# A decoder trunk on one Trainium2 core: three page buffers in the compression, and the attention projection with its narrow block first and its sample rows in halves

## The chip, the cores and the metric

The kernel runs on one core of one Trainium2 chip. The metric is the device time of one execution in microseconds. The core's engines work side by side and meet in semaphores: PE (TensorE, matrix products and transposes), ACT (ScalarE), DVE (VectorE), POOL (GpSimd) and SP (SyncE, which here only issues DMAs). ACT issues some DMAs as well, in the order of its own program.

## The reference

One layer of a decoder for 1024 prompt rows and 64 sample rows (8 sequences of 8 new tokens). What the change touches is the first projection and the compression of keys and values:

```python
z = rms_norm(x, norm1_g) @ w_in          # 1024 -> 1304 attention columns + 1664 RWKV columns
# attention columns: q (512) | 3 branches x (k, v) (768) | gates (24)

def compress_blocks(kv, cmp_pe, cmp_w):  # blocks of 32 tokens, stride 16
    chunks = kv[:, :n_chunks * 16].reshape(B, n_chunks, 16, 2, 2, 64)
    for i in range(2):
        part = chunks[:, i:i + n_cmp] + pe[:, i]
        comp = comp + einsum('bnscgd,csde->bncge', part, w[:, i])
```

`compress_blocks` is computed for the prompt (63 blocks) and for each of the 8 sample sequences over its 2048 cached tokens (127 blocks), whose 16 pages of 128 tokens lie scattered in a pool and are found through `page_table`. After that come the attention of the prompt and of the samples, the output projection and an MLP; the RWKV part (time mixing in chunks) lies between the projection and the compression.

## The kernel before

**Projection.** The 1088 rows of x are 9 tiles (`TILES`): 8 of 128 rows and one, number `PT` = 8, of 64 sample rows. For each tile SP loads x (`load_x`), ACT normalises it (`norm_rows`, two buffers `xn`), PE turns it in 8 transposes into PSUM banks 0 and 1 (`turn_x`), and DVE copies it out into `nt` (semaphore `nt_out`, L2023). The attention columns of `w_in` are three blocks (`BLOCKS`, L506): two of 512 columns and one of 280. `ATT` lists 27 groups, block by block and in a block tile by tile; `att_group` (L1320) computes one as 8 products over the contraction, `nt` stationary and the weights moving, into one of three PSUM banks, and ACT copies it to `za` (`att_out`, L917 to L926). SP loads blocks 0 and 1 at the start (`load_w`), block 2 into the buffer of block 0 once its 9 groups are done. PE's program runs the turns of tiles 0 and 1, then the groups of block 0 with one turn ahead of each, and then the rest. The head norms of DVE and ACT (`head_sums`, `head_scale`, `head_norm`) need all three blocks of a tile and run beside the third block and the first groups of the RWKV columns (`rw_group`), which follow.

**Compression.** It runs over `CSEQ`: step k = 0 is sample sequence 1, step 1 the prompt, steps 2 to 8 the other samples, each in two halves a (keys, values), so 18 halves (`CHALF`). The pages of a step are loaded into one of two page buffers, `page_rows[k % 2]`: even pages by SP (`load_pages`, L652), odd ones by ACT (`odd_pages`, L1125 to L1135, four pages at a time). DVE splits them into heads (`split_heads`, L2260 to L2266, two halves ahead), PE transposes (`cm_turn`, L1622), DVE and ACT copy the result to `xt` (`x_copy`, L2273 and L1112), PE multiplies with the weights (`cm_product`) and adds neighbours (`cm_select`), ACT stores keys and values (`kv_copy`). A page buffer is free once the heads of the step that used it before are split (`cm_heads`). ACT issues the odd pages of step k + 2 at the end of its work for the halves of step k. The second buffer is the place of sample states that SP has to store first (`stored`). `mixed` holds the attention output in its first four rows of tiles, empty at this point, and the RWKV output in the other four.

Each engine works through its program in order, and all waits are on counts of progress.

## Time and profile before

| | us |
|---|---|
| median of 3 timed runs | 2261.91 (2259.36 to 2263.99) |
| the profiled execution | 2249.74 |
| its span, first to last instruction | 2248.0 |
| PE busy | 2115.9 (94%) |
| DVE busy | 1128.7 (50%) |
| ACT busy | 628.5 (28%) |
| POOL busy | 150.7 (7%) |

PE's mean granted clock over the span was 0.979 of full speed. In the names of operations, `arena` is the large SBUF buffer in which nearly all tiles lie; a line number leads to the code. L1299 is the helper of all matmuls, so these are told apart by shape: 128*64 is the stationary operand (rows * columns), 128x512 the moving one. A float32 product appears as two instructions, so a group of 8 products is x16. In a timeline, rows of the same kind are merged (x4), the second number is their length together, and the bracket is the idle time of the engine before them. In a chain of waits, the second number is the share of time that the piece holds up the chain.

### The profile page before, as it was taken

The numbers are of one execution on the slowest core, as the hardware profiler recorded it, in microseconds if no ns is written. First come the engines' busy times: TensorE is split into PE (matmuls) and PEld (weight loads), VectorE is DVE, ScalarE is ACT, GpSimd is POOL, SyncE is SP. The second block draws the span as 40 slices with busy tenths as digits, with TensorE's granted clock in tenths as the row PEclk, the third lists the DMA queues.
The fourth block names the chain that finished last, engine by engine and source line by source line (L and its number), as shares of the span: only waits on it lengthen the run. The fifth ranks groups of instructions, "written<-read, shape, count | busy, mean of one in ns | idle before, by whom it ended". The sixth has DMA issues, their size and how long they took to land.

```text
span 2248.0 us, 36929 instructions
## 1 busy us (share of the span) xinstructions
PE 2115.9 (94%) x15228; PEld 1199.6 (53%) x15228; DVE 1128.7 (50%) x2278; ACT 628.5 (28%) x1408; POOL 150.7 (7%) x248
## 2 busy tenths in 40 slices
PE   7999999899998887888887899999999999999999
PEld 4456566799996774444344444444444444444443
DVE  2026664367665446766545313463636354554635
ACT  4113553222322115666543311202020111111110
POOL 3000000122222001211110000000000000000000
PEclk9999999999998997999998999999999999999999
DMA  6000112100012531000035421011111111111101
GB/s 189 21 1 19 29 29 88 68 4 22 4 23 77 170 96 54 10 5 5 5 113 154 129 75 61 11 60 42 38 38 38 38 38 38 38 38 38 38 38 80
DMA packets 99957, 115.72 MB, mean 51 GB/s; under 512 B 32243, under 2 KB 72116, under 8 KB 99726
## 3 DMA queue, kind: packets, MB, share of 16 engines
q1 hardware_dynamic: 95310, 106.01, 15.0%
q10 hardware_dynamic: 4480, 7.34, 1.1%
q8 instruction: 121, 1.98, 0.4%
q14 instruction: 46, 0.38, 0.1%
HBM read 104.75 MB, written 12.64 MB: 52 GB/s over the span
## 4 chain that ended last, share of the span: by engine, by line
PE 83%; DVE 6%; ACT 5%; DMA 2%; issue 2%; SPq 2%; ACTq 1%; POOL 0%; POOLq 0%; DVEq 0%
PE psum L1299 77%; PE psum L1724 2%; ACT arena L1182 2%; ACT arena L1168 1%; DMA arena<-in_cache_cmp_kv_dram 1%; SPq L702 1%; DVE arena L2343 1%; PE psum L1781 1%; PE psum L1622 1%; DVE arena L2369 1%; ACTq L1135 1%; DVE arena L2196 1%; DMA arena<-in_x_prompt_dram 0%; PE psum L1540 0%; SPq L646 0%
## 5 line engine op out<-in xcount | busy, mean ns | idle before, releaser
L1299 PE MATMUL psum<-arena 64*64 64x64 f32 (+12 forms) x12272 | 1863.6, 349 | 76.8 <-ACT arena L1182 44.0
L1299 PEld LDWEIGHTS psum<-arena 64*64 64x64 f32 (+5 forms) x12272 | 969.9, 152 | 872.5 <-issue 677.6
L2523 DVE TENSOR_TENSOR arena<-arena,psum 128x512 f32<-128x512 f32 x48 | 33.0, 688 | 305.8 <-PE psum L1299 305.8
L1280 ACT ACTIVATE arena<-psum 128x512 f32<-128x512 f32 x48 | 28.5, 594 | 420.0 <-PE psum L1299 327.3
L1271 ACT ACTIVATE arena<-arena 128x512 f32<-128x512 f32 x64 | 40.2, 628 | 274.2 <-DVE arena L2533 168.0
L1168 ACT ACTIVATE arena<-psum 128x512 f32<-128x512 f32 (+1 forms) x148 | 80.8, 595 | 86.3 <-PE psum L1724 74.4
L856 POOL TENSOR_TENSOR arena<-arena,m_lev 128x256 f32<-128x256 f32 x82 | 65.3, 797 | 586.2 <-DVE arena L2177 388.8
L1182 ACT ACTIVATE arena<-psum,arena 128x640 f32<-128x640 f32 (+7 forms) x128 | 88.8, 700 | 11.4 <-DVE arena L2343 10.9
L2343 DVE TENSOR_REDUCE arena<-psum 128x1 f32<-128x640 f32 (+7 forms) x128 | 84.6, 703 | 2.2
L2196 DVE TENSOR_TENSOR arena<-arena,psum 128x512 f32<-128x512 f32 x65 | 44.6, 687 | 74.2 <-PE psum L1299 73.5
L1048 ACT ACTIVATE arena<-psum 128x256 f32<-128x256 f32 x82 | 31.5, 384 | 171.4 <-PE psum L1299 171.4
L1724 PEld LDWEIGHTS psum<-ident,arena 128*128 128x128 f32 x528 | 59.1, 145 | 35.0 <-ACT arena L1168 15.4
L1724 PE MATMUL psum<-ident,arena 128*128 128x128 f32 x528 | 75.6, 288 | 2.1 <-DVE arena L2369 1.1
L2506 DVE TENSOR_TENSOR arena<-psum,arena 128x1024 f32<-128x1024 f32 x8 | 9.8, 1225 | 97.8 <-PE psum L1299 97.8
L1622 PE MATMUL psum<-ident,arena 128*128 128x128 f32 x272 | 42.6, 283 | 13.1 <-DVE arena L2266 13.1
L926 ACT ACTIVATE arena<-psum 128x512 f32<-128x512 f32 (+3 forms) x27 | 14.4, 532 | 133.2 <-PE psum L1299 133.2
L886 POOL TENSOR_SCALAR arena<-arena 128x640 f32<-128x640 f32 (+4 forms) x64 | 46.7, 741 | 49.1 <-DVE arena L2366 48.9
L1299 PE MATMUL psum<-ident,arena 64*64 64x64 f32 (+1 forms) x920 | 47.5, 223 | 2.5 <-DVE arena L2177 0.8
L1781 PE MATMUL psum<-ident,arena 128*128 128x128 f32 (+1 forms) x248 | 41.8, 307 | 8.4 <-DMA arena<-in_cache_slc_kv_dram 4.2
L2266 DVE COPY arena<-arena 128x512 f32<-128x512 f32 x68 | 27.9, 457 | 40.8 <-DMA arena<-in_cache_cmp_kv_dram 40.3
L1781 PEld LDWEIGHTS psum<-ident,arena 128*128 128x128 f32 (+1 forms) x248 | 29.5, 152 | 30.6 <-ACT arena L1217 14.6
L1299 PEld LDWEIGHTS psum<-ident,arena 64*64 64x64 f32 (+1 forms) x920 | 42.7, 139 | 4.4 <-DVE arena L2303 1.0
(311 smaller groups left out, 1717.8 us busy)
## 6 DMA issues: line engine op xcount, KB each, us to landing
arena<-in_cache_slc_kv_dram SPq DMA_DIRECT2D x128, 128.0 KB, 2.3
arena<-in_w_up_dram SPq DMA_DIRECT2D x7, 2048.0 KB, 7.4
arena<-in_w_down_dram SPq DMA_DIRECT2D x7, 2048.0 KB, 7.8
arena<-in_cache_cmp_kv_dram SPq DMA_DIRECT2D x72, 128.0 KB, 3.3
arena<-in_x_prompt_dram SPq DMA_DIRECT2D x16, 512.0 KB, 9.5
arena<-in_cache_cmp_kv_dram ACTq DMA_DIRECT2D x56, 128.0 KB, 3.1
arena<-in_w_in_dram SPq DMA_DIRECT2D x13, 512.0 KB, 3.9
arena<-in_w_in_dram SPq DMA_DIRECT2D x2, 2048.0 KB, 14.1
```

Source lines behind the costliest of these rows:

```text
L856: nc.gpsimd.tensor_tensor(amt[:, n % 2], atrb_r[c % 3][:, :, 0, :], spread(m_lev[:, i, :], 1, HP), ALU.mult).then_inc(sem("rw_amt"), 1)
L886: ins = nc.gpsimd.tensor_scalar(pb_w[:, h, 0:w], pb_w[:, h, 0:w], psum_[:, 1, h:h + 1], gates[:, i, 3 * h + 2:3 * h + 3], ALU.mult, ALU.mult)
L1168: nc.scalar.activation(ptb[2 * (st % 2) + g][0:p0], banks[4 + (f + g) % 2][0:p0], ACT.Copy).then_inc(sem("turn_out"), 1)
L1182: nc.scalar.activation((pb_w if br else pb_s)[:, h, 0:w], psum[:, s0:s0 + w], ACT.Exp, bias=pmax[:, br, h:h + 1], accum_out=psum_[:, br, h ...
L1271: link(nc.scalar.activation(block, block, ACT.Relu))
L1299: return nc.tensor.matmul(out, lhsT, rhs, start=start, stop=stop)
L1622: ins = nc.tensor.transpose(banks[g % 4][:, cols], by_head[a][x][:, cols], ident)
L1724: ins = nc.tensor.transpose(b[:, hh * P:(hh + 1) * P], (pb_w if s[0] else pb_s)[:, h, c0:c0 + P], ident)
L1781: ins = nc.tensor.transpose(b[0:t.shape[1], x * P:(x + 1) * P], t, ident)
L2196: tt(flat, flat, banks[4], ALU.subtract).then_inc(sem("rw_t"), 1)
L2343: nc.vector.tensor_reduce(pmax[:, br, h:h + 1], psum[:, s0[g]:s0[g] + w], AX.X, ALU.max, negate=True).then_inc(sem("pa_max"), 1)
L2523: tt(u2, t_sb, bank_of(6), ALU.add).then_inc(sem("u_sum"), 1)
```

## The change

- `page_rows` gets a third buffer, `mixed[:, 0:4]`, used by steps k % 3 == 1; the old second one is now for k % 3 == 2. Its semaphore is shared with the second half of the sample states (`S0_IN`, `PAGES_IN`, `pages_landed`).
- SP loads the prompt's pages (k = 1) right after `rw_all_done`, before it waits for the state's stores; its loads of k = 3 and on wait until the heads of step k - 3 are split, no longer those of step k - 2.
- ACT issues the odd pages of step k + 3 where it issued those of k + 2, and those of step 2 in addition during step 0, behind a wait for the state's stores.
- `BLOCKS` begins with the 280 columns. x tile 1 is loaded ahead of the weights, and `att_group(0)` runs ahead of `turn_x(1)`.
- For the 64 sample rows, each product of a group is two, one for each half of the columns, with outputs in the lower and the upper 64 partitions of the bank; ACT copies them out in two instructions.

```diff
@@ page buffers
-        page_rows = [[ft[:, slot + x, 0:SEQ] for x in range(HP)] for slot in (F_PR0, F_K)]
+        page_rows = [[rows_[:, slot + x, 0:SEQ] for x in range(HP)] for rows_, slot in ((ft, F_PR0), (mixed, 0), (ft, F_K))]
+        S0_IN = ("s0_in0", "s0_in1_then_pages_in2")
+        PAGES_IN = ("pages_in0", "pages_in1", S0_IN[1])
         def pages_landed(k):
-            return 16 * sum(4 if CSEQ[q] == 0 else NPG for q in range(k % 2, k + 1, 2))
+            return 16 * 4 * (k % 3 == 2) + 16 * sum(4 if CSEQ[q] == 0 else NPG for q in range(k % 3, k + 1, 3))
@@ blocks, x and weights
-        BLOCKS = [(0, 512), (512, 512), (1024, ZA - 1024)]
+        BLOCKS = [(1024, ZA - 1024), (0, 512), (512, 512)]
             load_x(0)
+            load_x(1)
             ...
             load_w(0)
-            for t in range(1, TILES):
+            for t in range(2, TILES):
                 load_x(t)
@@ SP, compression
+            sp.wait_ge(*once("rw_all_done"))
+            sp.wait_ge(sem("cmp_stored"), 16 * PT)
+            for t in range(SEQ // (2 * P)):
+                dst = page_rows[1][t // 2][:, 512 * (t % 2):512 * (t % 2) + 512]
+                sp.dma_start(dst, prompt_cmp[0, 0, 2 * t:2 * t + 2].rearrange(
+                    "n (c s) a g d -> (n c) (s a g d)", s=2)).then_inc(sem(PAGES_IN[1]), 16)
             sp.wait_ge(sem("shift_stored"), 64)
             sp.wait_ge(sem("stored"), 16 * stores[0])
-            sp.wait_ge(*once("rw_all_done"))
-            sp.wait_ge(sem("cmp_stored"), 16 * PT)
-            for k in range(1, NSEQ):
-                if CSEQ[k] == 0:
-                    ...
+            for k in range(2, NSEQ):
                 numbers = page_numbers(CSEQ[k], 2)
-                if k >= 2:
-                    sp.wait_ge(sem("cm_heads"), gbase(k - 1, 0))
+                if k >= 3:
+                    sp.wait_ge(sem("cm_heads"), gbase(k - 2, 0))
                 load_pages(k, numbers)
@@ ACT, att_out
+                if m == PT:
+                    for h, half in enumerate(HALVES):
+                        out, src = za[0:NS, m, c0 + h * n // 2:c0 + (h + 1) * n // 2], banks[2 + i % 3][half, 0:n // 2]
+                        if c0 == 0:
+                            out = za[0:NS, m, 0:n].rearrange("p (h g d) -> p g h d", g=KVH, d=HD)[:, h]
+                            src = src.rearrange("p (h d) -> p h d", d=HD)
+                        ins = nc.scalar.activation(out, src, ACT.Copy)
+                    ins.then_inc(sem("att_out"), 1)
+                    return
@@ ACT, odd_pages
-                if k >= 2 and first == 1:
-                    act.wait_ge(sem("cm_heads"), gbase(k - 1, 0))
+                if k == 2 and first == 1:
+                    act.wait_ge(sem("stored"), 16 * stores[1])
+                elif first == 1:
+                    act.wait_ge(sem("cm_heads"), gbase(k - 2, 0))
@@ ACT, loop over the halves
-                if k + 2 < NSEQ:
-                    odd_pages(k + 2, 1 + 8 * a)
+                if k == 0:
+                    odd_pages(2, 1 + 8 * a)
+                if k + 3 < NSEQ:
+                    odd_pages(k + 3, 1 + 8 * a)
@@ PE, att_group
+                if m == PT:
+                    for k in range(KT):
+                        for h, half in enumerate(HALVES):
+                            ins = mm(banks[2 + i % 3][half, 0:n // 2], nt[:, k, SEQ:], wb[b % 2][:, k, h * n // 2:(h + 1) * n // 2],
+                                     k == 0, k == KT - 1)
+                    ins.then_inc(sem("proj"), 1)
+                    return
@@ PE, start
             turn_x(0)
-            for t in range(TILES):
+            att_group(0)
+            turn_x(1)
+            for t in range(1, TILES):
                 if t + 1 < TILES:
                     turn_x(t + 1)
                 att_group(t)
```

Elsewhere `k % 2` of the page buffers becomes `k % 3`, and `s0_in` becomes `S0_IN`.

## Rows read from the trace of the kernel before

**Rows 1.** The page of the profile: busy time of each engine.

```profile
PE 2115.9 (94%) x15228; PEld 1199.6 (53%) x15228; DVE 1128.7 (50%) x2278; ACT 628.5 (28%) x1408; POOL 150.7 (7%) x248
```

**Rows 2.** Chain of waits, 0 to 60 us: start us, length us, what.

```profile
2.35 10.03 DMA arena<-in_x_prompt_dram
...
15.34 1.97 PE psum L1309 x8
17.31 7.34 PE psum L1299 x16
24.65 0.87 PE psum L1309 x8
25.52 6.87 PE psum L1299 x16
```

**Rows 3.** Timeline of the start: start us, us, engine, line, operation, shapes, [idle before].

```profile
7.74 1.94 PE L1309 MATMUL psum<-ident,arena 128*128 128x128 f32 x8 [7.74 <-ACT arena L907]
...
8.97 1.44 DVE L2023 TENSOR_TENSOR arena<-psum,g 128x512 f32<-128x512 f32 x2 [3.27 <-PE psum L1309]
```

**Rows 4.** DMA issues of the first and third weight block: KB, us to landing.

```profile
arena<-in_w_in_dram SPq DMA_DIRECT2D x1, 2048.0 KB, 9.4
...
arena<-in_w_in_dram SPq DMA_DIRECT2D x1, 1120.0 KB, 5.1
```

**Rows 5.** Busy time by stretch: stretch, its us, engines, then granted clock (PEclk).

```profile
86.70:182.30 95.60, 95.60 (x286) 52.49 (x286) 19.76 (x57) 9.82 (x23) 0.00 (x0) 1.00 0.04 12
182.30:408.30 226.00, 223.12 (x985) 135.21 (x984) 126.92 (x325) 99.46 (x266) 0.00 (x0) 1.00 0.18 55
...
788.40:793.50 5.10, 4.74 (x18) 3.51 (x18) 3.29 (x9) 0.61 (x1) 0.00 (x0) 0.67 0.30 96
```

**Rows 6.** Waits, 751.4 to 838.4 us: total us, times, longest.

```profile
DVE arena L2266 <- DMA arena<-in_cache_cmp_kv_dram: 35.1, 6, 6.6
```

**Rows 7.** Chain of waits, 715 to 860 us: the pages of sequence 2.

```profile
740.22 4.57 DMA arena<-in_cache_cmp_kv_dram
```

**Rows 8.** Timeline of ACT: two evictions of the narrow block.

```profile
152.88 0.40 ACT L926 ACTIVATE arena<-psum 128x280 f32<-128x280 f32 x1 [3.38 <-PE psum L1299]
156.65 0.40 ACT L926 ACTIVATE arena<-psum 128x280 f32<-128x280 f32 x1 [3.37 <-PE psum L1299]
```

**Rows 9.** Timeline of PE: the output projection's sample rows.

```profile
1396.79 7.09 PE L1299 MATMUL psum<-arena 128*64 128x512 f32 x32
```

**Rows 10.** Timeline of PE, compression, 738 to 839 us.

```profile
738.69 0.61 PE L1299 MATMUL psum<-arena 128*128 128x128 f32 x4
...
751.45 1.10 PE L1299 MATMUL psum<-arena 128*128 128x256 f32 x4
...
762.70 0.66 PE L1299 MATMUL psum<-arena,ident 128*64 128x127 f32 x8
763.29 0.66 PE L1622 MATMUL psum<-ident,arena 128*128 128x128 f32 x4
...
767.27 0.60 PE L1622 MATMUL psum<-ident,arena 128*128 128x128 f32 x4
...
768.58 0.99 PE L1299 MATMUL psum<-ident,arena 128*127 128x64 f32 x8
769.41 0.61 PE L1622 MATMUL psum<-ident,arena 128*128 128x128 f32 x4
...
838.43 1.03 PE L1299 MATMUL psum<-arena 128*128 128x256 f32 x4
```

**Rows 11.** Timeline of ACT, start of the compression (ACTq are its DMA issues).

```profile
732.45 0.61 ACT L1112 ACTIVATE arena<-psum 128x512 f32<-128x512 f32 x1 [2.01 <-PE psum L1622]
734.01 2.72 ACTq L1135 DMA_DIRECT2D arena<-in_cache_cmp_kv_dram  x4
...
737.16 0.59 ACT L1112 ACTIVATE arena<-psum 128x512 f32<-128x512 f32 x1
...
738.28 3.27 ACTq L1135 DMA_DIRECT2D arena<-in_cache_cmp_kv_dram  x4
```

More of the change, by code:

```diff
@@ L643, in _ @@
                 sp.dma_start(s0raw[b][0:64].rearrange("p (h k) -> p h k", h=HEADS),
-                             state_wkv[0, b].rearrange("h v k -> v h k")).then_inc(sem(f"s0_in{b // 4}"), 16)
+                             state_wkv[0, b].rearrange("h v k -> v h k")).then_inc(sem(S0_IN[b // 4]), 16)
             def page(b, n):
@@ L651, in load_pages @@
                     t = n // 2
-                    sp.dma_start(page_rows[k % 2][t // 2][HALVES[n % 2], 512 * (t % 2):512 * (t % 2) + 512], src).then_inc(sem(f"pages_in{k % 2}"), 16)
+                    sp.dma_start(page_rows[k % 3][t // 2][HALVES[n % 2], 512 * (t % 2):512 * (t % 2) + 512], src).then_inc(sem(PAGES_IN[k % 3]), 16)
             def page_numbers(u, step=1):
@@ L676, in _ @@
             stores.append(stores[0])
+            sp.wait_ge(*once("rw_all_done"))
+            sp.wait_ge(sem("cmp_stored"), 16 * PT)
+            assert CSEQ[1] == 0
+            for t in range(SEQ // (2 * P)):
+                dst = page_rows[1][t // 2][:, 512 * (t % 2):512 * (t % 2) + 512]
+                sp.dma_start(dst, prompt_cmp[0, 0, 2 * t:2 * t + 2].rearrange(
+                    "n (c s) a g d -> (n c) (s a g d)", s=2)).then_inc(sem(PAGES_IN[1]), 16)
             sp.wait_ge(sem("shift_stored"), 64)
             sp.wait_ge(sem("stored"), 16 * stores[0])
-            sp.wait_ge(*once("rw_all_done"))
-            sp.wait_ge(sem("cmp_stored"), 16 * PT)
-            for k in range(1, NSEQ):
-                if CSEQ[k] == 0:
-                    for t in range(SEQ // (2 * P)):
-                        dst = page_rows[k % 2][t // 2][:, 512 * (t % 2):512 * (t % 2) + 512]
-                        sp.dma_start(dst, prompt_cmp[0, 0, 2 * t:2 * t + 2].rearrange(
-                            "n (c s) a g d -> (n c) (s a g d)", s=2)).then_inc(sem(f"pages_in{k % 2}"), 16)
-                    continue
+            for k in range(2, NSEQ):
                 numbers = page_numbers(CSEQ[k], 2)
-                if k >= 2:
-                    sp.wait_ge(sem("cm_heads"), gbase(k - 1, 0))
+                if k >= 3:
+                    sp.wait_ge(sem("cm_heads"), gbase(k - 2, 0))
                 load_pages(k, numbers)
@@ L920, in att_out @@
                 c0, n = BLOCKS[b]
+                if m == PT:
[7 more added lines that the diff above has]
+                    return
                 out, src = za[0:rows(m), m, c0:c0 + n], banks[2 + i % 3][0:rows(m), 0:n]
-                if b == 0:
+                if c0 == 0:
                     out = out.rearrange("p (h g d) -> p g h d", g=KVH, d=HD)
@@ L1134, in odd_pages @@
                     t = n // 2
-                    act.dma_start(page_rows[k % 2][t // 2][HALVES[n % 2], 512 * (t % 2):512 * (t % 2) + 512], src).then_inc(sem(f"pages_in{k % 2}"), 16)
+                    act.dma_start(page_rows[k % 3][t // 2][HALVES[n % 2], 512 * (t % 2):512 * (t % 2) + 512], src).then_inc(sem(PAGES_IN[k % 3]), 16)
             for x in range(1, cgroups(0), 2):
@@ L1546, in s0_pe @@
                     if b % 4 == 0:
-                        pe.wait_ge(sem(f"s0_in{b // 4}"), 16 * 4)
+                        pe.wait_ge(sem(S0_IN[b // 4]), 16 * 4)
                     pe.wait_ge(sem("rw_prod_sb"), 2 * n + 2)
@@ L2261, in split_heads @@
                 if x == 0 and a == 0:
-                    dve.wait_ge(sem(f"pages_in{k % 2}"), pages_landed(k))
+                    dve.wait_ge(sem(PAGES_IN[k % 3]), pages_landed(k))
                 if k > 0:
                     dve.wait_ge(sem("cm_turned"), gbase(k - 1, a) + min(x + 1, cgroups(k - 1)))
-                tokens = shaped(page_rows[k % 2][x], 4, 2, KVH, HD)[:, :, a]
+                tokens = shaped(page_rows[k % 3][x], 4, 2, KVH, HD)[:, :, a]
                 nc.vector.tensor_copy(shaped(by_head[a][x], KVH, 4, HD).rearrange("p g t d -> p t g d"), tokens).then_inc(sem("cm_heads"), 1)
```

## The prediction

> **What bounds the kernel now.** I read the page first: TensorE (PE) is busy for 2115.9 us of a span of 2248.0 [rows 1]. A microsecond off this kernel is therefore either a gap in PE's work or PE work removed. Then I looked for gaps in the two stages that the diff touches.
>
> The start, by the chain of waits [rows 2] and the timeline [rows 3]. The second tile of x lands at 12.38, because it stands behind the 2 MB weight block in SP's queue; ACT normalises it; its turn on PE (`turn_x(1)`) runs at 15.34; only then comes the first group of the projection, at 17.31. The program orders it so: `att_group(0)` stands behind `turn_x(1)`. Its own inputs were there much earlier: tile 0 was turned at 7.74 and copied out by DVE by 10.41 [rows 3], and the weight block, issued just before the second x tile at 2.35 [rows 2], landed 9.4 us after its issue, by 11.7 [rows 4]. From 86.7 to 182.3 PE has no gap (nor in the chain from 17.31 on), and from 182.3 to 408.3 it is busy for 223.12 of 226.00 us [rows 5]: what is saved in the projection moves all that follows forward.
>
> The compression. DVE waits for cached pages in front of its head split (L2266) six times between 751.4 and 838.4, 35.1 us in all [rows 6], and once before. The chain goes through ACT's issues of the odd pages and then their flight, 4.57 us from the last issue for sequence 2 [rows 7]. ACT issues the last four pages of sequence k at the end of half (k-2, 1), and DVE wants them at the start of half (k-1, 0), the next one: too late by the time of issue plus flight. PE inherits part of each wait.
>
> **Part 1, start of the projection.** The narrow block (280 columns) goes first, x tile 1 is loaded ahead of it, and `att_group(0)` runs before `turn_x(1)`.
> - Earliest start. The first transfer on the queue is unchanged, so tile 0 is still copied out at 10.41. Ahead of the narrow block stand 2 x tiles (1 MB) and then its own 1.1 MB, 2.2 MB where old x0 and w0 were 2.6 MB; such a block alone takes 5.1 us from issue to landing [rows 4]. The old 2.6 MB was there by 11.7, and at the 2048 KB in 9.4 us of the first row 0.4 MB is up to 1.8 us. So it lands at 10 to 10.5, and the group starts at about 10.5; if the narrow block comes 1 us later than I think, the same is lost.
> - Its length: the narrow groups end 3.77 us apart [rows 8]. PE is cold at first. The old first turn and the old second turn took 1.94 and 1.97 us for what later takes 0.87 (24.65 to 25.52), and the first wide group 7.34 instead of 6.87 [rows 2, 3]. I charge 0.8 us here, between 0.2 and 1.7. It ends at 15.1.
> - `turn_x(1)` and `turn_x(2)` now follow each other directly, and the second needs the PSUM banks of the first, whose DVE copies take 1.44 for two [rows 3]. I charge 0.8 us of new stall. ACT needs 2.9 us for a tile (landing at 12.38 to turn at 15.34) and has just finished tile 0 at 7.7, so tile 1 is ready at about 10.6, long before 15.1.
> - Balance: old, turns 0 and 1 were done at 17.31 with 0.47 still to lose in the cold: 17.78. New: 15.1, less the 3.77 of the group that is already done, plus one turn 0.87, plus 0.8: 13.0. **Saved 4.8 us**, between 3.3 and 6.
>
> What is moved past: the two small issues behind it on SP (norm vector, x2 and on) shift by under 1 us, and tile 2 is wanted only after the group. ACT needs 2.9 us for a tile plus 0.40 for an eviction, against 3.77 + 0.87 of PE per tile, so ACT doesn't take over. `load_w` of the third block now waits for the end of a narrow block at about 52 us and has a wide block of 58 us to land in. DVE's head work still runs beside the third block, now 6.87 us a group instead of 3.77, so it has more room; its position against the following stage is the same. All at nothing.
>
> **Part 2, sample rows in halves.** The sample tile has 64 rows, so a group streams all columns through half of the array: 6.87 us, as for 128 rows. Now each matmul is split in two of half the columns in the two column halves of the array. The trace has this form in the output projection: 32 matmuls of 128*64 with 512 columns take 7.09 us, 0.22 each [rows 9], where the full ones take 6.87 / 16 = 0.43 [rows 2]. So two run at once. With 256 columns I get 32 x 0.107 = 3.4, with 140 columns 32 x 0.058 = 1.9. The nearest row to a short one is the selection of the compression: 8 matmuls of 127 columns in 0.59 (762.70 to 763.29), 0.074 each, where half of 0.107 would be 0.053 [rows 10], so some 0.02 is added. I take 3.6 and 2.4. Saved: 2 x (6.87 - 3.6) + (3.77 - 2.4) = **7.9 us**, between 6.2 and 8.4. The second eviction on ACT (0.40) hides under PE.
> By the Trainium skill, "TensorEngine Tiling (Array Packing)", section "Instruction Overhead", each matmul carries about 60 cycles, and a tiling factor shouldn't be taken from a dimension that is small. Added in full to 32 matmuls that is an estimate of 0.8 us a group by that page, and the sum of this part would be some 5.5; the 0.59 us row agrees with a cost of that size for the shortest form only, the 7.09 us row shows next to none.
>
> **Part 3, third page buffer, steady state.** Loads of sequence k are now issued one whole sequence earlier. PE work of one sequence, free of stalls [rows 10]: 8 pairs of a turn and a product at 1.31 (767.27 to 768.58), selections 0.59 (762.70 to 763.29) and 0.83 (768.58 to 769.41), about 0.15 for changes of form: 12.05 us. Now the first product of sequence 2 starts at 751.45 and that of sequence 8 at 838.43: 86.98 for six, 14.5 each. The surplus is 86.98 - 72.3 = 14.7 us; it holds the gaps, slow restarts behind them, and one stretch at a granted clock of 0.67 (a mix of the 1.2 and the 2.4 GHz level, behind a gap) from 788.4 to 793.5 [rows 5]. With pages a sequence early, all of it can go: DVE's and ACT's own work, page issues included, already kept up with PE in the stretch without stalls around 763 to 771.
>
> **Part 4, what it costs at its start.** In its first two halves ACT used to issue the odd pages of sequence 2; now it issues those of 2 and 3, eight more. One batch takes 0.95 from the end of the copy before (733.06) to the first issue, where the page numbers are read, and 2.72: 3.67; the four issues of the next took 3.27 [rows 11], and some reading ahead of them. I take 3.6. Queued behind the first extra batch: the copy for product (1, 0), at 737.16 [rows 11]; PE starts that product at 738.69 [rows 10], so 0.9 us are covered and PE stalls for 2.7. Behind that stand the last pages of sequence 2, which were the bound already (they land at 744.8 [rows 7]): they go out 3.6 us later, and so land 3.6 later, at 748.4. The second extra batch stands in front of the copy for (1, 1), done at about 749.2, when the first turn on the new pages is about done too. The two delays don't add: **3.6 us lost**, between 0 and 6. SP issues its prompt loads ahead of its wait for the state's stores instead of behind it, but PE has work at that point, so that gives nothing; DVE waits for the same stores ahead of its own splits for the products that PE runs before 734.01, so the new wait of ACT on `stored` is met when ACT comes to it. SP's eight extra even pages stand only in front of later pages. Behind that point every wait of the stages is on progress, so the gain isn't taken back.
> The Trainium skill says ("DMA: Bandwidth & Descriptors", "Issuing engines are not separate DMA queues") that issuing from several engines saves only sequencer time, usually small beside the transfer. Here four issues take 2.72 to 3.27 us beside a flight of 4.57, so the trace disagrees with "small". If it held, part 4 would cost nothing.
>
> **Sum.** 4.8 + 7.9 + 14.7 - 3.6 = 23.8 us. The profiled execution took 2249.7, so its successor should take about 2226. The median of the timed runs is 2261.9, 12 us above it, and I take the same difference off that: **2238 us**.
>
> **Rivals.**
> - The halves don't run at once with short columns: part 2 gives nothing, 2246. For it: no row with 128*64 and 256 columns. Against: the 7.09 us row. 8%.
> - Short matmuls carry more than I charge: 0.02 us on each of 32, as in the 0.59 us row, gives groups of 4.1 and 2.5 and a part 2 of 6.8; twice that gives 4.7, 3.2 and 4.9. So 2239 to 2241, say 2240. For it: that row. Against: the long form of the 7.09 us row, to which 256 columns are as near. 9%. It is also what the rule of the tiling page of the Trainium skill would do; the trace bears it out in the 0.59 us row only.
> - The early issues cost nothing (ACT's page numbers and issues slip into its idle time): 2234. Against: the chain goes through exactly these issues [rows 7, 11]. 6%.
> - The change doesn't do what it says in the compression: pages still arrive late because transfers, not their issue, are the limit. Then part 3 gives 0 and part 4 stays: 12.7 - 3.6 = 9.1, 2253. For it: a flight of 4.57 us. Against: 2 MB in 12 us is far below what 2048 KB in 9.4 us shows [rows 4]. 8%.
> - Slower: a denser PE is granted a lower clock in the long rest. The place is all of PE's 2115.9 us; it decides from 23.8 / 2116 = 1.1% less clock on; with 3% less the time is about 2238 + 63 = 2300. For it: the clock isn't 1.00 throughout. Against: the low stretches follow gaps, as at 788.4, and the 95.6 us without a gap have 1.00 [rows 5]. 3%.
>
> **How the numbers follow.** Forecast 66%. Its bounds: projection 9.5 to 14.4, compression 8 to 14.7, so 17.5 to 29 us of gain, 2233 to 2244. With 2246 and the spread of the timed runs I say 2232 to 2248. A measurement of this kernel can tell about 0.2%, 4.5 us, from no change; all cases but the last are faster by more, though 2253 is near enough that I leave a little for "same": faster 0.94, same 0.03, slower 0.03.
>
> **What would show it.** Right: the first product on PE at about 10.5, narrow groups first, the last eviction of the projection 12.7 us earlier than before; 32 matmuls of 256 columns in 3.4 to 3.7 us; in the compression a PE gap of about 2.7 us before product (1, 0), DVE waiting for pages only at sequence 2, and about 12.05 us per sequence behind it; the prompt attention some 24 us earlier. Wrong: waits of DVE for pages at sequences 3 to 8, a PE gap in the narrow groups (ACT late), or the first product waiting for weights beyond 12.

## The result and the profile after

| | before | after |
|---|---|---|
| median of the timed runs, us | 2260.64 (4 runs, 2255.53 to 2263.99) | 2227.53 (4 runs, 2225.07 to 2237.53) |
| the profiled execution, us | 2249.74 | 2225.07 |
| its span, us | 2248.0 | 2223.3 |

The ratio after to before is 0.9866, with a 95% interval of 0.9838 to 0.9894: the change saves 24 to 37 us. The prediction was 2238 with a range of 2232 to 2248, so the kernel came out faster than the range allowed. But the two profiled executions lie 24.7 us apart, and the predicted sum was 23.8. That contradiction is the subject of what follows.

(Line 503 holds `BLOCKS` in the kernel before; the text ahead of the prediction gives the number that it has after the change.)

The page of the profile after, busy time of each engine, to be held against [rows 1]:

```profile
span 2223.3 us, 37028 instructions
PE 2105.2 (95%) x15276; PEld 1198.1 (54%) x15276; DVE 1128.6 (51%) x2278; ACT 628.7 (28%) x1411; POOL 151.2 (7%) x248
```

PE's busy time fell by 10.7 us (2115.9 to 2105.2), and the other 14.0 of the 24.7 were gaps.

**The start.** The chain of waits after, from 0 to 60 (columns: start us, us, what), answers to [rows 2, 3]:

```profile
7.70 1.96 PE psum L1324 x8
9.68 0.70 DVE arena L2047
10.52 5.74 PE psum L1314 x16
16.27 0.45 PE psum L1324 x4
16.74 0.70 DVE arena L2047
17.58 1.16 PE psum L1324 x8
18.74 3.77 PE psum L1314 x16
22.51 0.87 PE psum L1324 x8
23.39 3.78 PE psum L1314 x16
...
46.40 6.03 PE psum L1314 x48
```

The first product runs at 10.52, as predicted. The first narrow group, though, takes 5.74 us, where later ones take 3.77: 2.0 us for the cold start instead of the 0.8 that I charged (upper bound 1.7). The turns of tiles 1 and 2 then follow each other with a wait for DVE between them, and from 18.74 on a group and a turn alternate without a gap. The last row holds the narrow group of tile 7 (16 matmuls) and that of the sample tile (32); what the halves save on it is read further down, beside the same row without them.

**The end of the projection.** ACT's timeline, evictions of the last two groups (the last column is the idle time before, and who ended it):

```profile
167.24 0.60 ACT L937 ACTIVATE arena<-psum 128x512 f32<-128x512 f32 x1 [5.83 <-PE psum L1314]
170.85 0.77 ACT L929 ACTIVATE arena<-psum 64x256 f32<-64x256 f32 x2 [3.02 <-PE psum L1314]
```

The last group of the sample rows comes 3.61 us behind the one before it (predicted: 3.6). The last eviction starts at 170.85; before it was 183.21. That is 12.4 us earlier (predicted: 12.7).

**The compression.** What DVE waits for (columns: waited for, us in total, times, longest us), and the chain of waits from 708 to 741, to be held against [rows 6, 7, 10, 11]:

```profile
DVE arena L2290 <- DMA arena<-in_cache_cmp_kv_dram: 8.7, 1, 8.7
```

```profile
716.78 0.44 PE psum L1646 x4
...
718.56 0.48 ACT arena L1123
719.07 0.32 ACTq L1140
...
726.61 0.50 ACTq L1148
...
727.63 0.26 ACT arena L1123
...
729.94 0.50 ACTq L1148
730.60 3.76 DMA arena<-in_cache_cmp_kv_dram
734.38 0.44 DVE arena L2290
734.86 0.66 PE psum L1646 x4
```

The timelines of ACT (its issues) and PE (product (1, 0)):

```profile
720.16 6.95 ACTq L1148 DMA_DIRECT2D arena<-in_cache_cmp_kv_dram  x8
```

```profile
728.23 1.19 PE L1314 MATMUL psum<-arena 128*128 128x128 f32 x4 [3.26 <-issue]
```

DVE waits for pages once, at sequence 2, and not seven times. The price at the start is there too. ACT issues eight pages (L1148; L1140 reads their numbers) between its copies of 718.56 and 727.63; PE waits 3.3 us for the second copy, ahead of product (1, 0). The last page of sequence 2 is issued at 729.94, and the turn on it runs at 734.86. Behind that PE has hardly a gap. The windows view of 740 to 820 (columns: length, busy us and instructions of PE, PEld, DVE, ACT, POOL, then granted clock, DMA share, GB/s):

```profile
740.00:820.00 80.00, 79.77 (x528) 68.56 (x525) 40.73 (x91) 18.91 (x40) 0.00 (x0) 1.00 0.40 115
```

So each step of the sum can be seen, and for this pair of executions the sum is right. The question for the experiments was: why do the medians differ by more than these two traces?

### The profile page after: what moved, and what is told of

Read it like the earlier page. It is cut to its first block, busy times and chain, and to the rows that moved or that the text cites. A ratio compares the mean times of both kernels' runs of the same rounds, so it can differ in the third digit from the quotient of the medians.

```text
span 2223.3 us, 37028 instructions
## 1 busy us (share of the span) xinstructions
PE 2105.2 (95%) x15276; PEld 1198.1 (54%) x15276; DVE 1128.6 (51%) x2278; ACT 628.7 (28%) x1411; POOL 151.2 (7%) x248
## 4 chain that ended last, share of the span: by engine, by line
PE 86%; DVE 5%; ACT 5%; issue 2%; SPq 1%; DMA 1%; ACTq 0%; POOL 0%; POOLq 0%; DVEq 0%
PE psum L1314 79%; PE psum L1748 2%; ACT arena L1197 2%; ACT arena L1183 2%; PE psum L1646 1%; PE psum L1805 1%; DVE arena L2367 1%; DVE arena L2393 1%; SPq L704 1%; DVE arena L2220 1%; PE psum L1564 0%; PE psum L1324 0%; SPq L650 0%; DVE psum L2364 0%; ACTq L1148 0%
## 5 line engine op out<-in xcount | busy, mean ns | idle before, releaser
L1314 PE MATMUL psum<-arena 64*64 64x64 f32 (+10 forms) x12320 | 1856.3, 348 | 80.1 <-ACT arena L1197 44.9
L1183 ACT ACTIVATE arena<-psum 128x512 f32<-128x512 f32 (+1 forms) x148 | 80.7, 596 | 88.4 <-PE psum L1748 76.7
L1197 ACT ACTIVATE arena<-psum,arena 128x640 f32<-128x640 f32 (+7 forms) x128 | 88.9, 701 | 10.9 <-DVE arena L2367 10.6
L937 ACT ACTIVATE arena<-psum 128x512 f32<-128x512 f32 (+1 forms) x24 | 12.8, 533 | 116.2 <-PE psum L1314 116.2
L2364 DVE TENSOR_TENSOR psum<-psum,edge_causal 128x256 f32<-128x256 f32 x48 | 20.6, 428 | 46.2 <-PE psum L1314 45.9
L1646 PE MATMUL psum<-ident,arena 128*128 128x128 f32 x272 | 41.4, 277 | 1.6 <-DVE arena L2290 1.6
```

The costliest lines, as they stand in the source:

```text
L1183: nc.scalar.activation(ptb[2 * (st % 2) + g][0:p0], banks[4 + (f + g) % 2][0:p0], ACT.Copy).then_inc(sem("turn_out"), 1)
L1197: nc.scalar.activation((pb_w if br else pb_s)[:, h, 0:w], psum[:, s0:s0 + w], ACT.Exp, bias=pmax[:, br, h:h + 1], accum_out=psum_[:, br, h ...
L1314: return nc.tensor.matmul(out, lhsT, rhs, start=start, stop=stop)
L1646: ins = nc.tensor.transpose(banks[g % 4][:, cols], by_head[a][x][:, cols], ident)
```

## The experiments

**Theories.** (The recorded expectations letter their own theories anew.) A: the saving in a typical execution is larger than in this pair, because the trace of before from which I sized the gaps was a mild one. B: the saving is the 24.7 us of the pair, and the medians differ by chance. Beside these, each part was tried alone, and the start cost of the compression (part 4) was taken apart.

### The kernel before, again

No edit.

> The kernel before, unchanged, as a control. The profiled execution of it took 2249.7 us, its timed runs 2255.5 to 2264.0. Theory A (the spread belongs to the execution, whatever the kernel): ratio 1.000, its timed runs again between 2250 and 2265 with the granted clock lower in the longer ones, and its profiled execution somewhere in that range, not at its lower end for a reason. Theory B (the profiled execution is always the fast one): profiled 2249 to 2251 again, timed runs again some 12 us above it.

Measured: 2257.32 (12 runs, 2246.47 to 2262.88), ratio to the other runs of before 0.9995 (0.9978 to 1.0012). Beside the other experiments the kernel before was timed 39 times more, 2249.96 to 2265.45, median 2259.14, standard deviation 3.7. My profiled execution of 2249.74 is below all 39 and below 11 of the 12 runs here, so it lies at the fast end without being the fastest. Of this run's own two theories the second falls, as the profiled execution took 2260.38 this time; the first holds but for its range, which the lowest run leaves.

The same stretch in more traces of before. What DVE waits for, from 735 to 850 (with the first wait, which [rows 6] left out), in the profiled execution and in a third trace (`before_third`):

```profile
DVE arena L2266 <- DMA arena<-in_cache_cmp_kv_dram: 40.3, 7, 6.6
```

```profile
DVE arena L2266 <- DMA arena<-in_cache_cmp_kv_dram: 42.2, 7, 6.8
```

The waits hardly differ. I now take the stretch that the prediction took, from the first product of sequence 2 to that of sequence 8. In `before_again` it runs from 754.21 to 844.53, in `before_third` from 755.53 to 846.16. The windows view of it, for the profiled execution of before, `before_again` and `before_third`, in this order:

```profile
751.45:838.43 86.98, 76.76 (x483) 63.10 (x482) 36.98 (x85) 17.30 (x36) 0.00 (x0) 0.98 0.44 128
```

```profile
754.21:844.53 90.32, 79.80 (x482) 65.41 (x481) 36.93 (x85) 17.29 (x36) 0.00 (x0) 0.94 0.43 123
```

```profile
755.53:846.16 90.63, 79.88 (x483) 65.11 (x481) 36.97 (x85) 17.32 (x36) 0.00 (x0) 0.94 0.42 123
```

The work is the same (482 or 483 matmuls), and so is PE's idle time within 0.6 us (10.2, 10.5 and 10.8). But PE is busy for 3.0 to 3.1 us longer in the other two, at a granted clock of 0.94 against 0.98. That is nearly all of the 3.3 and 3.6 us by which the stretch is longer. The low stretches stand behind the gaps. The chain of waits of `before_third` at the first of them:

```profile
743.30 4.62 DMA arena<-in_cache_cmp_kv_dram
747.94 0.44 DVE arena L2266
748.38 0.04 issue
748.42 1.11 PE psum L1622 x4
749.54 0.85 PE psum L1299 x4
750.39 0.85 PE psum L1622 x4
751.24 1.49 PE psum L1299 x12
```

A turn of four transposes takes 0.85 here and 0.44 in the undisturbed stretch at 716.78 that the changed kernel's chain shows above: after the gap PE runs at the 1.2 GHz level for a while. In my trace that happened behind one gap of this stretch [rows 5], in the others behind three each. The third trace of before had its own expectation:

> The kernel before, once more, for a further look at its compression, which took 126.1 and 131.4 us in its first two traces. Theory (each gap for pages is followed by a stretch at a low granted clock in some executions and not in others, so the stage varies): between 126 and 136 us, and with it the mean stays at 130 or more. Rival (126.1 is the rule and 131.4 a single disturbance): 126 to 127 us.

Measured: 132.0 us for the compression, and the mean of the three is 129.8, just under the expected 130. The rival falls.

### Stage by stage, in 14 traces

The stages are cut at the first instruction of a PE line: the first turn of the compression (L1622 before, L1646 after), of the prompt attention (L1677, L1701), of the sample attention (L1759, L1783) and of the output projection (L1969, L1993), and the last matmul. For instance (one line of the program: duration min/median/max in ns, first and last start), `before_third` and the changed kernel:

```profile
L1622 PE MATMUL psum<-ident,arena x272: 270/273/476, 726.5 to 850.8; 128*128 128x128 f32 x136
```

```profile
L1646 PE MATMUL psum<-ident,arena x272: 270/272/421, 710.8 to 817.4; 128*128 128x128 f32 x136
```

Lengths in us:

| kernel | up to the compression | compression | prompt attention | sample attention | rest |
|---|---|---|---|---|---|
| before | 724.7 | 126.1 | 299.4 | 157.9 | 934.3 |
| before_again | 725.5 | 131.4 | 300.2 | 161.7 | 934.3 |
| before_third | 726.5 | 132.0 | 303.2 | 161.7 | 934.3 |
| project_only | 710.5 | 135.0 | 299.9 | 158.0 | 934.3 |
| project_again | 715.5 | 130.9 | 297.1 | 161.8 | 934.3 |
| half_pages | 727.3 | 111.7 | 303.1 | 158.5 | 934.3 |
| compress_only | 726.1 | 116.9 | 302.8 | 159.9 | 934.3 |
| after | 710.8 | 114.3 | 299.9 | 158.4 | 934.3 |
| after_again | 710.6 | 116.3 | 295.5 | 160.4 | 934.3 |
| halves_off | 721.7 | 117.1 | 304.3 | 162.0 | 934.3 |
| sp_step2 | 710.8 | 114.4 | 303.1 | 161.9 | 934.3 |
| sp_step3 | 716.2 | 113.5 | 302.8 | 160.3 | 934.3 |
| sp_step3_again | 711.1 | 112.5 | 302.6 | 159.9 | 934.3 |
| sp_step2_early | 716.2 | 107.3 | 297.2 | 161.5 | 934.3 |

With two buffers and all pages (the first five rows) the compression takes 126.1 to 135.0, mean 131.1. With three and ACT's issues as in the change (compress_only, after, after_again, halves_off) it takes 114.3 to 117.1, mean 116.2. So the third buffer, its start cost included, is worth 14.9 us on the mean, and 11.8 in the pair that I had. The two sets don't overlap, so the gain is sure; its size is less so, as the first five scatter by 9 us and the 14.9 is uncertain by some 3 (an estimate from their scatter). In the attention stages nothing differs that could be told from their scatter (295.5 to 304.3 and 157.9 to 162.0).

### Each half of the change alone

`compress_only` leaves the projection as before; `project_only` leaves the compression as before. The core of the edits, against the changed kernel:

```diff
-        BLOCKS = [(1024, ZA - 1024), (0, 512), (512, 512)]
+        BLOCKS = [(0, 512), (512, 512), (1024, ZA - 1024)]
...
-                if m == PT:
-                    for k in range(KT):
-                        for h, half in enumerate(HALVES):
...
-             att_group(0)
-             turn_x(1)
-             for t in range(1, TILES):
+             for t in range(TILES):
```

> Only the compression part of the change (third page buffer and its loads); the projection is as before. Theory A (each part gives what the two traces show, and the other 6 us of the timed difference are spread): 11.8 us, ratio 0.9948. Theory B (the page gaps of the kernel before cost more in ordinary executions than in the profiled one, since PE is at the low clock behind more of them): 17 to 20 us, ratio 0.992. In the trace both expect the PE stall of 3.3 us ahead of product (1, 0) and no waits for pages from step 3 on.

Measured: 2244.88 (6 runs, 2235.01 to 2247.73), ratio 0.9937 (0.9915 to 0.996). The interval holds both 0.9948 and 0.992, so this run doesn't decide between its two theories. DVE waits for pages once, at sequence 2; PE's stall ahead of product (1, 0) is 2.7 us and not 3.3.

> Only the projection part (narrow block first, x tile 1 ahead of the weights, first group ahead of the second turn, sample rows in halves); compression as before. Theory A: 13 to 14 us, ratio 0.9940. Theory B, in which only the gaps of the compression differ between executions: the same 13 to 14 us here, and the rest in the compression. A third theory, that the projection's gain is larger than the trace shows because the cold start differs: 18 us or more, ratio 0.992.

Measured: 2249.54 (12 runs, 2238.55 to 2253.59), ratio 0.9955 (0.9938 to 0.9973). That holds the expected 0.9940 and excludes the third theory's 0.992. Its second trace:

> The kernel with the projection's changes alone, once more: two page buffers, as before. Theory: its compression, unchanged by the edit, took 135.0 us in its first trace, and takes 126 to 136 again; the stretch up to the compression is 710.5 to 716.5 us. Rival (the spread belongs to the kernel, which starts the stage earlier): 135 again within 1 us.

Measured: 130.9 us for the compression and 715.5 up to it. So the 135.0 of the first trace was scatter, not an effect of the earlier start. The two ratios multiply to 0.9892, the change has 0.9866: within the intervals the parts add up. Taken by itself, though, 0.9892 is 24.4 us, the very number of the rival that the saving is the pair's 24.7. By the stage table they bring 14.9 and 13.3 us (726.0, the mean of five traces without the projection's changes, less 712.7, the mean of eight with all of them), 28.2 in all.

### The changed kernel, again

> The changed kernel once more, unaltered. The question is whether the error of the prediction was the size of the saving or its conversion from one profiled execution to a median. Theory (conversion): single executions of one kernel lie 4 to 5 us apart (standard deviation), and the 12 us between the profiled execution and the median was such a distance; then the median of many is 2227 to 2232, the kernel before beside it again about 2258, ratio 0.986 to 0.989. Rival (the saving itself is about 34 us, as the first two medians say): 2224 to 2227, ratio 0.984 to 0.985. In the compression: 114 to 117 us from its first turn to the first turn of the prompt attention under both.

Measured: 2228.19 (4 runs, 2224.42 to 2228.93), beside the kernel before at 2258.84; ratio 0.9867 (0.9849 to 0.9884); its compression took 116.3 us. Theory B of the start of this section, that the saving is the pair's 24.7, is put aside by a little: the lower end of this saving, 0.0116 of 2259, is 26 us, and 24.7 lies outside; it lay just inside the first interval (24 to 37), and the two parts timed alone came to it. A is borne out by the stage table and by the stretch shown above, although 2259.1 - 28.2 = 2230.9 is still 3 us above the two medians. Of this run's own two expectations the median and the ratio fit the first.

### Half the pages, with two buffers

The kernel before, without the odd pages of sequences 3 to 8:

```diff
-                if k + 2 < NSEQ:
+                if k == 0:
                     odd_pages(k + 2, 1 + 8 * a)
```

The count of landed pages that DVE waits for is lowered to match.

> The kernel before (two buffers), in which from the third cached sequence on only the even pages are loaded; the odd halves of the rows keep what stood there, so the compressed keys and values of those sequences are computed from the wrong rows: the loads of the odd pages are left out, and all of PE's, DVE's and ACT's own work is kept. Theory (the gaps of the compression in the kernel before are waits for pages, bound by ACT's late issues and their flight, and nothing else differs): the page gaps of sequences 3 to 8 go, 12.0 us per sequence, the compression from its first turn to the first turn of the prompt attention takes 111 to 114 us where the kernel before has 126 to 135, so 15 to 20 us less; 2238 to 2245 us in all. Rival (two buffers also hold up the even pages' issues, or DVE or ACT limits the stage): over 120 us, 2248 or more. Rival (the saving of the third buffer is the 11.8 us of the first pair of traces): about 12 us less, 2246.

Measured: 2242.55 (4 runs, 2241.48 to 2245.26), ratio 0.9924 (0.9901 to 0.9947), 17 us less than before; the compression takes 111.7, and DVE waits for pages once:

```profile
DVE arena L2266 <- DMA arena<-in_cache_cmp_kv_dram: 5.7, 1, 5.7
```

PE's, DVE's and ACT's computing is all there, the third buffer is not, and the stage is 19 us shorter than the mean of the five traces with two buffers. So the surplus of before was waits for late pages and what follows on them. By itself this run can't tell late issues from slow transfers, as it also moves half the bytes and frees ACT of its issues; the change itself does that, since it moves all pages and still has DVE wait once only.

### The projection without the halves

The changed kernel with the sample rows as full-width products again (the two `if m == PT` branches of the diff taken out).

> The changed kernel without the halves: the sample rows are projected as full-width products again. Theory: the sample groups take 6.87 (wide) and 3.77 us (narrow) and not 3.6 and 2.3, so the projection's last eviction comes 7.9 to 8.4 us later than in the changed kernel, 178.7 to 179.3, and the stretch up to the compression is 718.7 to 719.3 us long. Rival (part of the 12.4 us at the start is not the halves' but the block order's): less than 7 us later.

Measured, ACT's timeline of its last two groups:

```profile
173.09 0.60 ACT L928 ACTIVATE arena<-psum 128x512 f32<-128x512 f32 x1 [5.83 <-PE psum L1305]
180.10 0.59 ACT L928 ACTIVATE arena<-psum 64x512 f32<-64x512 f32 x1 [6.41 <-PE psum L1305]
```

A wide sample group comes 7.01 us behind the last one, 3.61 with the halves: 3.40 saved, twice. For the narrow one the chain of waits has this row, where the changed kernel has 6.03:

```profile
46.98 7.89 PE psum L1305 x32
```

That is 1.86 saved, nearly half of 3.77. In sum 8.7 us (predicted 7.9). The last eviction, at 180.10, comes 8.0 to 9.7 us later than in the eight traces with halves (170.43 to 172.09). The stretch up to the compression, at 721.7, lies outside the expected 718.7 to 719.3, which left no room for its scatter: in the eight traces with halves it is 710.5 to 716.2.

What is left for the block order: the last eviction starts at 183.21 to 185.04 in five traces without the projection's changes (mean 184.2) and at 171.1 on the mean with them; 13.1 - 8.7 = 4.4 us (predicted 4.8, of which the cold group took 1.2 more than I charged). The first trace alone would give 12.4 - 8.7 = 3.7.

### Part 4: what the early issues cost

SP instead of ACT issues the odd pages of sequence 2 (`sp_step2`, the diff here; ACT's wait for the state's stores goes with them), or of sequence 3 (`sp_step3`, further down):

```diff
-                numbers = page_numbers(CSEQ[k], 2)
+                numbers = page_numbers(CSEQ[k], 1 if k == 2 else 2)
...
-                if k == 0:
-                    odd_pages(2, 1 + 8 * a)
```

> The changed kernel, but SP issues all 16 pages of step 2, so ACT issues only the four odd pages of step 3 per half at the start, as many as in the kernel before. If the doubled issues on ACT cost what the forecast says: PE's stall of 3.3 us ahead of product (1, 0) is gone, the pages of step 2 are there at about the time that PE wants them, and the kernel gains 3.5 to 7 us on the changed one (ratio to before 0.984). If the delay at the start comes from something else (the pages' flight, DVE's gates in between): under 1 us.

Measured: 2232.47 (4 runs, 2231.4 to 2233.23), ratio 0.9891 (0.9869 to 0.9914), compression 114.4. ACT's stall ahead of product (1, 0) is gone, yet nothing is won. The chain of waits shows SP in its place:

```profile
711.72 0.28 SPq L650
712.00 0.03 issue
712.04 0.29 SPq L650
...
716.13 0.26 SPq L650
...
716.59 0.55 SPq L656
...
727.40 6.82 DMA arena<-in_cache_cmp_kv_dram
```

Behind its wait for the stores SP reads 16 page numbers, about 0.29 us each, and only then issues the first page, at 716.59, 5.8 us into the stage. The last page was under way by 727.40, 3.2 us before the change's, but took 6.82 us and not 3.76, so it landed at about the same time, 734.2; why it took longer wasn't tried. The expected gain of 3.5 to 7 us didn't come. `sp_step2_early` reads them ahead of the wait:

```diff
+            step2 = page_numbers(CSEQ[2])
...
-                numbers = page_numbers(CSEQ[k], 1 if k == 2 else 2)
+                numbers = step2 if k == 2 else page_numbers(CSEQ[k], 2)
```

> The changed kernel, in which SP issues all 16 pages of the second cached sequence (ACT issues none of them) and reads their numbers before it waits for the states, not behind it. Theory (the PE gap ahead of the turn for product (2, 0) is bound by SP's own instructions: 16 page numbers of 0.29 us and 16 issues of 0.65 us behind the wait): the first issue goes out at about 711.8 and not 716.6, the last at about 722.6, the pages are there by 729.5, the PE gap of 6.67 us falls to 0 to 2, and the compression is 4.5 to 6 us shorter than with the numbers read late; 2224 to 2227 us. Rival (the transfers are the limit, 2 MB beside the state's transfers): the last page lands at the same 734 and the gap stays at 5 to 7 us; 2230 to 2232.

Measured: 2220.82 (5 runs, 2218.3 to 2225.15), ratio 0.9832 (0.9814 to 0.9851). SP's timeline:

```profile
714.88 2.13 SPq L687 DMA_DIRECT2D arena<-out_dram  x4
717.28 19.16 SPq L656 DMA_DIRECT2D arena<-in_cache_cmp_kv_dram  x23
```

The stage starts at 716.2 in this trace, so the first page goes out 1.1 us into it instead of 5.8. The compression takes 107.3 us, 7.1 less than with the numbers read late and 7.0 less than in the first trace of the change, more than the expected 4.5 to 6. DVE's waits for pages are down to 3.1 us, the PE gap of 6.67 is gone, and PE's granted clock is 1.00 over the first 40 us of the stage (with the numbers read late it is 0.91 there, and 0.91 in the change). The first issue is 4.7 us earlier; that the other 2.4 come from the higher clock is likely but not shown. The rival of the transfers falls. This is the fastest version of all, 7 us under the change; the two intervals just about meet (0.9851 and 0.9849).

In `sp_step3` ACT keeps its wait for the state's stores and the odd pages of sequence 2:

```diff
-                numbers = page_numbers(CSEQ[k], 2)
+                numbers = page_numbers(CSEQ[k], 1 if k == 3 else 2)
...
-                if k + 3 < NSEQ:
+                if 1 <= k and k + 3 < NSEQ:
                     odd_pages(k + 3, 1 + 8 * a)
```

> The changed kernel, in which SP issues all 16 pages of the third cached sequence; ACT issues the eight odd pages of the second sequence in the first two halves of the compression, as the kernel before did, and none of the third there. Theory (part 4 of the prediction: the second batch of four issues ahead of the copy is what stalls product (1, 0)): no PE stall of 3.3 us ahead of product (1, 0), the last odd pages of the second sequence issued about 3.6 us earlier, the turn for product (2, 0) at about 731 and not 734.9, the compression about 3.6 us shorter, 110.5 to 112. Rival (the stall comes from the new wait for the state's stores in front of ACT): the stall stays, and the compression is within 1 us of 114.3.

Measured, one execution: 2234.42; compression 113.5. ACT's timeline:

```profile
724.00 0.61 ACT L1123 ACTIVATE arena<-psum 128x512 f32<-128x512 f32 x1 [2.00 <-PE psum L1646]
725.56 3.47 ACTq L1148 DMA_DIRECT2D arena<-in_cache_cmp_kv_dram  x4
...
730.58 2.42 ACTq L1148 DMA_DIRECT2D arena<-in_cache_cmp_kv_dram  x4
```

Four issues between the copies and not eight, and no stall ahead of product (1, 0). So the stall came from the doubled issues and not from ACT's new wait, which is still there. The stage starts at 716.2 here. The turn for (2, 0) starts 21.9 us into it (738.11); in the changed kernel it is 24.1 (734.86 - 710.8). That is 2.2 us, less than the 3.5 that the last issue is earlier (its flight starts 16.3 us into the stage, at 732.51, against 19.8), as the flight took 5.09 us and not 3.76. The expectation of the next run puts this at 2.7 to 3.2; it is 2.2 and 3.2 against the two traces of the change.

> The changed kernel with all 16 pages of the third cached sequence issued by SP, timed now. Its first trace had no stall ahead of product (1, 0), and the turn for (2, 0) came 2.7 to 3.2 us earlier after the stage's start than in the two traces of the changed kernel, but then lay in a stretch with a granted clock of 0.66. Theory (the cost of the early issues was 3 to 3.6 us, and the clock of single executions hid it): the median of many is 2 to 4 us below that of the changed kernel, 2224 to 2226. Rival (the clock behind the one gap that is left takes it back each time): 2228 within 1.

Measured: 2231.88 (4 runs, 2227.74 to 2234.11), ratio 0.9877 (0.9855 to 0.99), compression 112.5. By the stage the two traces are 3.2 us shorter than the mean of the four with ACT's early issues (113.0 against 116.2), and the turn for (2, 0) starts 21.4 us into it on the mean, against 25.0 in those four. By the whole time there is no gain, the median is even 3.7 us above the change's, with intervals that overlap. So neither expectation on the median came true, and a cost of 3 us at this place is seen in the stage only.

## Why the prediction was wrong

- **Start, block order: right.** First product at 10.5; predicted 4.8, measured 4.4 on the mean (3.7 in the first trace), within the bounds of 3.3 to 6. The cold group's 0.8 was mis-sized (2.0).
- **Halves: right, a little undersized.** Predicted 7.9, measured 8.7, just above the bounds of 6.2 to 8.4. The groups were 3.6 and 2.4 in the prediction; less what was saved they are 6.87 - 3.40 = 3.47 and 3.77 - 1.86 = 1.91. The rival of the short matmuls falls: the Trainium skill's 60 cycles for each matmul ("TensorEngine Tiling (Array Packing)", "Instruction Overhead"), added in full by an estimate of 0.8 us a group, would have made the saving 5.5. The groups are within 0.1 us of the bare 3.4 and 1.9, so next to nothing of that cost is seen, and my own 0.2 and 0.5 on top were too much as well.
- **Third buffer: the mechanism right, the size wrong.** This is the term of the sum that was mis-sized. I took the surplus, 86.98 - 72.3 = 14.7 us, from one execution at the fast end. The same stretch, from the first product of sequence 2 to that of sequence 8, takes 90.32 and 90.63 us in the other two traces of before, and 94.08 and 89.95 in the two of `project_only`. So the surplus is 18.0, 18.3, 21.8 and 17.7 there, and 18.1 on the mean of all five. The waits themselves were the same (40.3 and 42.2 us); PE ran at its lower level behind more of the gaps than in my trace. The stall-free length was right: in the first trace of the change these six sequences take 72.2 us (740.56 to 812.73), 12.03 each for the predicted 12.05. Less the 3.6 of part 4 I had 11.1, and in the pair of traces it was 11.8; between five traces and four the stage saves 14.9.
- **Early issues: right within an us.** Predicted 3.6, as a stall of 2.7 and pages 3.6 later. The stall is 3.3 (2.7 to 3.5 in four traces), the turn on the pages comes 3.6 later, and the stage without the extra issues is 3.2 shorter. The rival "cost nothing" falls by the stage, though the whole time shows no gain. The Trainium skill's sentence that issuing costs only sequencer time, usually small ("DMA: Bandwidth & Descriptors", "Issuing engines are not separate DMA queues"), doesn't hold for issues in a row: ACT's eight took 6.95 us beside a flight of 3.76, and PE waited for the copy behind them.
- **From the profiled execution to the median: wrong. This is the step that failed.** I took 12 us off as a constant, and so supposed that the saving is the same in an execution of 2250 us as in one of 2262. For the two profiled executions the sum was right (2226 predicted, 2225.07 measured), but the second lies only 2.5 us below its kernel's first median. Part of the 12 us was the very cost that the change removes: the other two traces of before are 10.6 and 15.3 us longer than mine, 5.3 and 5.9 of it in the compression. This and the size of the third buffer's term are one error, a sum read from one short execution and carried to the median.

The miss is 2238 - 2227.5 = 10.5 us. Of it 2.8 is the start (2261.9 from three runs, where 39 give 2259.1), 4.4 the sizes (28.2 and not 23.8; 3.8 of it in the compression). The last 3.3 aren't settled: single runs of one kernel have a standard deviation of 1 to 5 us, and a median of four or eight of them can be that far off. A part of it may sit in the attention stages, whose means can't be told apart here. So the mis-sized term alone doesn't carry the number out of the range: with the stage table's 28.2 the same sum would have given 2261.9 - 28.2 = 2233.7, inside it.

The range was wrong for the same reason. Its upper bound for the compression was the 14.7 of this one execution with nothing taken off for part 4, as if an execution that loses more at its gaps were impossible.

## What to carry to other kernels

A profiled execution is one draw. Hold its time against all timed runs first; where it lies at the fast end, the gaps that you read in it may be a mild form of those gaps, and closing them may save more than it shows. Removing a gap can be worth more than its length, as here PE ran at its lower clock for some us behind several of them.

Where a page is late, look at what the issuing engine does between its wait and the first issue. Numbers read behind a wait that could be read ahead of it were worth more here than moving issues from one engine to another.

## What the runs showed of the hardware

- The same program, stage by stage, scattered where PE has gaps. The last 934.3 us, of which PE is busy for all but 0.5 of 930 in the trace of before (1310 to 2240), are the same to 0.1 us in all 14 traces; the compression scatters by 9 us with gaps (five traces) and by 3 without most of them (four traces).
- The stretch up to the compression took 710.5 to 711.1 us in five traces with all of the projection's changes and 715.5 to 716.2 in the other three. The windows of 670 to 680, just ahead of the chunk work's end, show it (the changed kernel, then `sp_step3`):

```profile
670.00:680.00 10.00, 8.75 (x257) 8.28 (x259) 5.21 (x14) 2.01 (x6) 0.00 (x0) 0.98 0.59 172
```

```profile
670.00:680.00 10.00, 8.03 (x155) 7.54 (x155) 3.53 (x7) 1.02 (x3) 0.71 (x1) 0.66 0.62 183
```

  One execution had a granted clock of 0.98 and the other 0.66 in the same ten us, at nearly the same point of the work (the second was 1.2 us behind from the start on), and 5.4 us separate them at the start of the compression, those 1.2 included. What decides between the two wasn't tried.
- A register read of a page number took 0.26 to 0.29 us on SP, and an issue of 128 KB 0.6 to 0.9 on ACT (2.42 and 3.47 for four) and up to 0.83 on SP (19.16 for 23, with waits among them).
